# Input stage of a hybrid encoder: order of loads, normalisation and first products

## What is computed

```python
h = layer_norm(x, ln_in_g, ln_in_b)      # (1024, 1024)
p = h @ w_in[0]                          # input projection
# three mixers on parts of p (RWKV-7, neighbourhood attention, latent attention)
# output projection, layer_norm, SwiGLU feed-forward, layer_norm
```

## Time and profile before

| | us |
|---|---|
| median of 3 runs | 1622.75 (1621.57 to 1623.96) |
| the profiled execution | 1622.15 |
| its span | 1620.3 |
| TensorE busy | 1537.1 (95%) |
| VectorE busy | 1074.8 (66%) |
| ScalarE busy | 626.1 (39%) |

### The profile page before, as it was taken

How to read it: one execution, slowest core, us unless ns; L and a number is a source line. 1 busy time by engine, 2 the same in 40 slices (tenths; PEclk the granted TensorE clock), 3 DMA queues, 4 the chain that set the end, 5 groups by cost and what they waited for, 6 DMA issues and landing times.

```text
span 1620.3 us, 25771 instructions
## 1 busy us (share of the span) xinstructions
PE 1537.1 (95%) x10160; PEld 1111.9 (69%) x10160; DVE 1074.8 (66%) x1508; ACT 626.1 (39%) x1157; POOL 360.8 (22%) x360
## 2 busy tenths in 40 slices
PE   4999998989899998999999998999999999998998
PEld 3788784655455545777764456888888888887786
DVE  6524598778756675767647579775555555688877
ACT  2212235655444434444431116333333333343453
POOL 0630004137400017888840050220000000000000
PEclk9999999999999999999999999999999999999999
DMA  6131010010000000000024011332321111755322
GB/s 237 40 152 42 13 53 8 1 33 13 12 12 12 19 11 21 3 2 29 2 77 171 1 52 52 110 111 82 97 95 53 53 53 53 257 197 182 127 69 105
DMA packets 28537, 109.78 MB, mean 68 GB/s; under 512 B 3488, under 2 KB 5888, under 8 KB 26256
## 3 DMA queue, kind: packets, MB, share of 16 engines
q1 hardware_dynamic: 27968, 103.05, 18.8%
q0 software_dynamic: 464, 5.28, 0.9%
HBM read 89.36 MB, written 18.92 MB: 67 GB/s over the span
## 4 chain that ended last, share of the span: by engine, by line
PE 84%; DVE 8%; POOL 3%; issue 2%; ACT 2%; DMA 1%; SPq 0%; DVEq 0%; POOLq 0%; ACTq 0%
PE psum L2746 26%; PE psum L2763 11%; PE psum L2252 9%; PE psum L2669 7%; PE psum L2419 5%; PE psum L2446 3%; PE psum L2343 2%; PE psum L2360 2%; PE psum L2314 2%; PE psum L2281 1%; PE psum L2453 1%; PE psum L2262 1%; PE psum L2643 1%; PE psum L2556 1%; PE psum L2538 1%
## 5 line engine op out<-in xcount | busy, mean ns | idle before, releaser
L2746 PE MATMUL psum<-h_hi,part_hi 128*128 128x512 f32 x616 | 166.3, 392 | 7.9 <-DVE arena L1937 4.6
L1884 DVE TENSOR_TENSOR part_lo<-arena,part_hi 128x512 fp32r<-128x512 f32 x154 | 118.0, 770 | 79.3 <-ACT part_hi L1210 79.0
L2746 PE MATMUL psum<-h_lo,part_hi 128*128 128x512 f32 x616 | 165.4, 390 | 0.0
L2746 PE MATMUL psum<-h_hi,part_lo 128*128 128x512 f32 x616 | 164.7, 389 | 0.0
L1210 ACT ACTIVATE part_hi<-arena 128x512 fp32r<-128x512 f32 x154 | 96.0, 628 | 134.8 <-PE psum L2746 119.1
L2746 PEld LDWEIGHTS psum<-h_hi,part_hi 128*128 128x128 f32 x616 | 115.9, 189 | 33.2 <-DVE arena L1937 5.1
L2746 PEld LDWEIGHTS psum<-h_lo,part_hi 128*128 128x128 f32 x616 | 116.2, 189 | 24.3
L2746 PEld LDWEIGHTS psum<-h_hi,part_lo 128*128 128x128 f32 x616 | 115.7, 188 | 24.1
L893 POOL TENSOR_TENSOR arena<-arena,consts 128x512 f32<-128x512 f32 x64 | 81.7, 1297 | 178.8 <-ACT arena L1114 178.2
L1559 DVE TENSOR_REDUCE stats<-psum 128x1 f32<-128x1024 f32 x64 | 77.8, 1216 | 50.5 <-PE psum L2343 50.4
L2669 PE MATMUL psum<-arena 128*128 128x512 f32 x256 | 110.5, 592 | 0.0
(11 more groups left out here) (322 smaller groups left out, 3078.2 us busy)
## 6 DMA issues: line engine op xcount, KB each, us to landing
arena<-in_w_gate SPq DMA_DIRECT2D x22, 512.0 KB, 3.6
arena<-in_w_up SPq DMA_DIRECT2D x22, 512.0 KB, 4.0
arena<-in_w_down SPq DMA_DIRECT2D x22, 512.0 KB, 3.8
arena<-in_w_down SPq DMA_DIRECT2D x11, 1024.0 KB, 4.9
arena<-in_w_in SPq DMA_DIRECT2D x15, 512.0 KB, 3.5
arena<-act_spill SPq DMA_DIRECT2D x12, 512.0 KB, 7.0
act_spill<-arena SPq DMA_DIRECT2D x10, 512.0 KB, 5.9
arena<-in_x SPq DMA_DIRECT2D x8, 512.0 KB, 11.2
```

The costliest lines, as they stand in the source:

```text
L1884: v.tensor_tensor(lo, raw[:, at:at + HALF], hi, ALU.subtract).then_inc(part_lo, 1)
L2746: mm = pe.matmul(bank({2: z, 3: y, 5: y}.get(p, x)), w[:, P * k:P * k + P], h[k // 2][:, HALF * (k % 2):HALF * (k % 2) + HALF], start=(fre ...
```

## The change

SyncE loads x tiles 0 to 3, each with its own semaphore, then both weight tiles, then x tiles 4 to 7 in pairs, then the constants and the value weights. GpSimd issues the two broadcast rows only when the last x tile is there. Statistics go by pairs of tiles. ScalarE normalises tiles 0, 1, 4 and 6 (by scale and bias, for which VectorE computes minus mean times reciprocal), VectorE 2, 3, 5 and 7. TensorE turns tile by tile, eight blocks each. In the first half ScalarE copies all blocks out, in the second VectorE three of them. VectorE takes the statistics of tiles 4 to 7 between the low parts of the first half. The two weight tiles are interleaved in the first half; in the second half blocks 6 and 7 are turned behind the first products, and the last five products of tile 1 stand behind the last of tile 0. The other edits set the counts of waits further on.

```diff
+IN_BANKS = ((0, 2, 1, 3, 4, 5, 6, 7), (1, 3, 4, 5, 6, 7, 4, 5))
+NORMED_BY_ACT, NORMED_BY_DVE = (0, 1, 4, 6), (2, 3, 5, 7)
+TURNED_BY_DVE = [(1, 1), (1, 4), (1, 7)]
+TURNED_BY_ACT = [(hf, k) for hf in range(NH) for k in range(KT) if (hf, k) not in TURNED_BY_DVE]
+IN_TURNS = (len(TURNED_BY_ACT), len(TURNED_BY_DVE))
...
-            for t in range(NT):
-                sp.dma_start(resid[:, t, :], a["x"][t]).then_inc(rows_in_place[t // 2], 16)
+            for t in range(4):
+                sp.dma_start(resid[:, t, :], a["x"][t]).then_inc(rows_in_place[t], 16)
                 if t == 0:
                     sp.dma_start(ident, a["consts"][:, 0:P]).then_inc(ident_in, 16)
-            sp.dma_start(w_raw[0], a["w_in"][0]).then_inc(weights_in[0], 16)
+            for s in range(NSLOT):
+                sp.dma_start(w_raw[s], a["w_in"][s]).then_inc(weights_in[s], 16)
+            for t in range(4, NT):
+                sp.dma_start(resid[:, t, :], a["x"][t]).then_inc(late_rows_in[t // 2 - 2], 16)
             sp.dma_start(consts[:, P:], a["consts"][:, P:]).then_inc(const_in, 16)
-            sp.dma_start(w_raw[1], a["w_in"][1]).then_inc(weights_in[1], 16)
...
             pool.dma_start(par[:, :], a["params"]).then_inc(par_in, 16)
+            pool.memset(proj[:, 0:NSHIFT, 0:1], 0.0).then_inc(pads, 1)
+            pool.memset(proj[:, 0:NSHIFT, T + 1:T + 2], 0.0).then_inc(pads, 1)
+            pool.wait_ge(late_rows_in[1], 32)
             pool.dma_start(g_row, a["rows"][0:1, :].partition_broadcast(P)).then_inc(rows_in, 16)
             pool.dma_start(b_row, a["rows"][1:2, :].partition_broadcast(P)).then_inc(rows_in, 16)
-            pool.memset(proj[:, 0:NSHIFT, 0:1], 0.0).then_inc(pads, 1)
-            pool.memset(proj[:, 0:NSHIFT, T + 1:T + 2], 0.0).then_inc(pads, 1)
...
-            def sd_in(hf):
-                act.wait_ge(var_ready, hf + 1)
-                act.activation(sd[:, 4 * hf:4 * hf + 4], mv[:, 4 * hf:4 * hf + 4, 1], ACT.Sqrt).then_inc(sd_ready, 1)
+            def sd_in(n):
+                act.wait_ge(var_ready, 2 * n + 1)
+                act.activation(sd[:, 2 * n:2 * n + 2], mv[:, 2 * n:2 * n + 2, 1], ACT.Sqrt).then_inc(sd_ready, 1)
+            def normalise_in(t):
+                act.wait_ge(var_ready, 2 * (t // 2) + 2)
+                act.activation(resid[:, t, :], resid[:, t, :], ACT.Identity, bias=less_means[:, t:t + 1],
+                               scale=rs[:, t:t + 1]).then_inc(norm_act, 1)
...
+            def turn_in(hf, k):
+                if 8 * hf + k >= 4:
+                    act.wait_ge(h_lo_ready, 8 * hf + k - 3)
+                act.wait_ge(ln_tr, 8 * hf + k + 1)
+                act.activation(h_tmp[k % 4], bank(IN_BANKS[hf][k]), ACT.Identity,
+                               bias=pcol("ln_in_b", k), scale=pcol("ln_in_g", k)).then_inc(h_tmp_ready[0], 1)
+            def hi_in(hf, k):
+                turned_in(act, hf, k)
+                act.activation(h_hi[k][:, hf * HALF:(hf + 1) * HALF], h_tmp[k % 4], ACT.Copy).then_inc(h_hi_ready, 1)
+            sd_in(0)
+            normalise_in(0)
+            sd_in(1)
+            normalise_in(1)
+            for j in range(NSLOT):
+                p_hi(j)
+            act.wait_ge(par_in, 16)
+            turn_in(0, 0)
+            turn_in(0, 1)
+            for k in range(KT):
+                hi_in(0, k)
+                if k + 2 < KT:
+                    turn_in(0, k + 2)
+                if k == 5:
+                    sd_in(2)
+            normalise_in(4)
+            sd_in(3)
+            normalise_in(6)
+            turn_in(1, 0)
+            for k in range(KT):
+                hi_in(1, k)
+                if (1, k + 2) in TURNED_BY_ACT:
+                    turn_in(1, k + 2)
...
+            def stats_in(t, j):
+                if t < 4:
+                    v.wait_ge(rows_in_place[t], 16)
+                else:
+                    v.wait_ge(late_rows_in[t // 2 - 2], 32)
+                own.add(v.bn_stats(bn[:, t, 6 * j:6 * j + 6], resid[:, t, j * HALF:(j + 1) * HALF]))
+                if j:
                     own.wait()
                     own.add(v.bn_aggr(mv[:, t, :], bn[:, t, :]))
+            def variance_in(n):
                 own.wait()
...
+                v.tensor_scalar(mv[:, 2 * n:2 * n + 2, 1], mv[:, 2 * n:2 * n + 2, 1], LN_EPS, None, ALU.add).then_inc(var_ready, 1)
+            def scale_in_of(n):
+                v.wait_ge(sd_ready, n + 1)
+                own.add(v.reciprocal(rs[:, 2 * n:2 * n + 2], sd[:, 2 * n:2 * n + 2]))
                 own.wait()
...
+                v.scalar_tensor_tensor(out=less_means[:, 2 * n:2 * n + 2], in0=mv[:, 2 * n:2 * n + 2, 0], scalar=-1.0,
+                                       in1=rs[:, 2 * n:2 * n + 2], op0=ALU.mult, op1=ALU.mult).then_inc(var_ready, 1)
+            def normalise_in(t):
+                v.tensor_scalar(resid[:, t, :], resid[:, t, :], mv[:, t, 0:1], rs[:, t:t + 1],
+                                ALU.subtract, ALU.mult).then_inc(norm_ready, 1)
+            def turn_in(hf, k):
+                v.wait_ge(h_lo_ready, 8 * hf + k - 3)
+                v.wait_ge(ln_tr, 8 * hf + k + 1)
+                v.tensor_scalar(h_tmp[k % 4], bank(IN_BANKS[hf][k]), pcol("ln_in_g", k),
+                                pcol("ln_in_b", k), ALU.mult, ALU.add).then_inc(h_tmp_ready[1], 1)
+            def lo_in(hf, k):
+                v.wait_ge(h_hi_ready, 8 * hf + k + 1)
+                v.tensor_tensor(h_lo[k][:, hf * HALF:(hf + 1) * HALF], h_tmp[k % 4],
+                                h_hi[k][:, hf * HALF:(hf + 1) * HALF], ALU.subtract).then_inc(h_lo_ready, 1)
...
-            for hf in range(2):
-                normalise_in(hf)
-                if hf == 0:
-                    v.wait_ge(par_in, 16)
-                    p_lo(0)
-                for k in range(0, KT, 2):
-                    v.wait_ge(ln_tr, 8 * hf + k + 2)
-                    v.tensor_scalar(h_tmp[k % 4 + 1], bank(5 + k % 4 if hf else k + 1), pcol("ln_in_g", k + 1),
-                                    pcol("ln_in_b", k + 1), ALU.mult, ALU.add).then_inc(h_tmp_ready[1], 1)
-                    for j in range(k, k + 2):
-                        v.wait_ge(h_hi_ready, 8 * hf + j + 1)
-                        v.tensor_tensor(h_lo[j][:, hf * HALF:(hf + 1) * HALF], h_tmp[j % 4],
-                                        h_hi[j][:, hf * HALF:(hf + 1) * HALF], ALU.subtract).then_inc(h_lo_ready, 1)
-                if hf == 0:
-                    p_lo(1)
+            for t in range(2):
+                for j in range(2):
+                    stats_in(t, j)
+            variance_in(0)
+            stats_in(2, 0)
+            scale_in_of(0)
+            stats_in(2, 1)
+            for j in range(2):
+                stats_in(3, j)
+            variance_in(1)
+            scale_in_of(1)
+            for t in range(2, 4):
+                normalise_in(t)
+            for j in range(NSLOT):
+                p_lo(j)
+            for k in range(KT):
+                lo_in(0, k)
+                if 1 <= k <= 4:
+                    stats_in(4 + (k - 1) // 2, (k - 1) % 2)
+                if k == 4:
+                    variance_in(2)
+                elif k == 5:
+                    scale_in_of(2)
+                if k > 4:
+                    stats_in(4 + (k - 1) // 2, (k - 1) % 2)
+            stats_in(7, 1)
+            variance_in(3)
+            normalise_in(5)
+            scale_in_of(3)
+            normalise_in(7)
+            v.wait_ge(par_in, 16)
+            turn_in(1, 1)
+            for k in range(KT):
+                lo_in(1, k)
+                if (1, k + 3) in TURNED_BY_DVE:
+                    turn_in(1, k + 3)
...
+            def normed(t):
+                if t in NORMED_BY_ACT:
+                    pe.wait_ge(norm_act, NORMED_BY_ACT.index(t) + 1)
+                else:
+                    pe.wait_ge(norm_ready, NORMED_BY_DVE.index(t) + 1)
+            def turn_in(hf, t, ks):
+                for k in ks:
+                    mm = pe.transpose(psum[:, IN_BANKS[hf][k], P * (t % 4):P * (t % 4) + P],
+                                      resid[:, t, k * P:(k + 1) * P], ident)
+                    if t % 4 == 3:
+                        mm.then_inc(ln_tr, 1)
+            def first_project(hf, b, k):
                 pe.wait_ge(p_lo_ready, b + 1)
+                pe.wait_ge(h_lo_ready, 8 * hf + k + 1)
                 w_hi_b, w_lo_b = w_parts[b]
...
+                for n, (w, x) in enumerate(((w_hi_b, h_hi), (w_hi_b, h_lo), (w_lo_b, h_hi))):
+                    mm = pe.matmul(bank(2 * b + hf), w[:, P * k:P * k + P], x[k][:, hf * HALF:(hf + 1) * HALF],
+                                   start=(k == 0 and n == 0), stop=(k == KT - 1 and n == 2), skip_group_check=True)
+                if hf and k == KT - 1:
+                    mm.then_inc(proj_done, 1)
             pe.sem_inc(proj_done, NSLOT)
...
+            for t in range(4):
+                normed(t)
+                turn_in(0, t, range(KT))
```

(54 more changed lines are left out.)

53 lines of the change are left out of this document (14 added, 39 removed).

## The result

| | before | after |
|---|---|---|
| median | 1622.34 us (1621.57 to 1623.96, 4 runs) | 1612.37 us (1611.72 to 1613.58, 4 runs) |
| span of the profiled execution | 1620.3 us | 1610.7 us |
| first matmul of weight tile 2 | 60.10 us | 50.19 us |

The ratio is 0.9936, 95% interval 0.9921 to 0.9951: 10.0 us faster. A later comparison on one chip, in which after ran five times beside other kernels, gave 1612.67 against 1620.04 us (11 runs), ratio 0.9956 (0.9943 to 0.9969). Both lie clear of 1, but the second gain is 7.4 us (5 to 9 by its interval) against 10.0 (8 to 13); which is nearer is open.

A forecast was written before the change was run, and what follows sets the result against it. The input stage's chain to weight tile 2's first matmul was taken as the bound, with TensorE waiting on VectorE's normalises. -4.5 - 1.9 - 0.8 - 4.5 + 2.3 = -9.4 (9.5 unrounded): 1622.75 - 9.5 = 1613.2 us, range 1610 to 1618.

The forecast's parts named there:

- to the first turn: Start until ScalarE's first copy of a transposed column out of PSUM: at 17.1 us instead of 21.65, -4.5.
- first turn to first matmul: Two turns, a rounding and a low part before TensorE's first product: 2.8 us instead of 4.7, -1.9.
- first half's products: Sixteen products of 0.70 us and one hole of 0.5: 11.7 us instead of 12.5, -0.8.
- between the halves: TensorE's stretch without products: 5.1 us instead of 9.6, -4.5, with tile 7 normalised and turned last.
- second half's products: Products 11.2 us, eight moved transposes 1.0, a hole 0.5, then a wait of 1.2: 13.9, +2.3.
- Tile 1's landing: x tile 1 in at 6.4 us, behind identity and parameters; bounds 5.8 at the best rate and 9.7 as today.
- The low clock: Seventeen transposes ahead of the first turn priced at 0.24 us each, the 1.2 GHz price, done at 16.9.
- Rival 2: TensorE's clock rises only at 26 us: tile 2 at 53.0; high from the first transpose: 48.7. Chance 0.13.
- The new wait: Weight tile 2 reuses tile 0's parts, freed at its last product: TensorE idle 1.2 us, low part taking 2.48.
- Rival 1: x tiles land as late as today, 9.7 and 13.78: tile 2 starts at 54.4, -5.7; chance 0.12.
- Rival 3: TensorE's clock never rises in the input stage, every matmul 0.47 us: tile 2 at 73.5, +13.4; chance 0.05.
- Rival 4: The gain is given back after the input stage, by other last-ending work or clock dips: about 1621; chance 0.08.

The follow-up runs named there:

- rows_first: after with GpSimd issuing the two row broadcasts at the start again, right behind the parameters; first matmul of weight tile 2 at 52.62 us against 50.19.
- par_late: after with the parameters' load issued only when x tile 1 is in; first matmul of weight tile 2 at 49.86 us against 50.19.
- ident_late: after with the identity loaded behind x tile 3 instead of x tile 0; weight tile 2 at 48.06 us; timed later, median 1610.83 us, ratio 0.9943 to before.
- pool_later: after with GpSimd starting its chain on the normalised rows only when weight tile 2 is split; first matmul of weight tile 2 at 49.83 us against 50.19.
- after_again: The unchanged kernel after, timed and traced a second time; median 1612.67 us, ratio 0.9956 to before, first matmul of weight tile 2 at 49.22 us.
- all_faster: after with identity behind x tile 3, parameters issued once x tile 1 is in, and x tile 5 normalised by ScalarE; median 1612.44 us, ratio 0.9947 to before.
- no_interleave: after with the first half's products as before: all eight blocks with weight tile 0, then with weight tile 1; weight tile 2 at 55.72 us against 50.19.
- warm_start: all_faster plus 18 unread products of a constant tile on TensorE ahead of everything; median 1609.04 us, ratio 0.9930 to before.
- norm_dve: after with all eight x tiles normalised by VectorE, none by ScalarE; first matmul of weight tile 2 at 54.48 us against 50.19.
- weights_late: after with the two weight tiles loaded behind x tiles 4 to 7; first matmul of weight tile 2 at 53.95 us against 50.19.

## Why the prediction was right

Forecast 1613.2 us, measured 1612.4 (a change of -9.5 forecast, -10.0 measured; in the later comparison -7.4); landmark forecast at 50.6, measured 50.19. The sum by its own terms:

| stretch | forecast | measured in after |
|---|---|---|
| to the first turn | -4.5 (at 17.1) | -3.9 (17.78) |
| first turn to first matmul | -1.9 (2.8 us) | -1.9 (2.83) |
| first half's products | -0.8 (11.7) | -0.9 (11.67) |
| between the halves | -4.5 (5.1) | -4.6 (5.03) |
| second half's products | +2.3 (13.9) | +1.3 (12.88) |

Three of the five were right within 0.1 us, since every price in them had a row. Of the two others one came out 0.7 us worse than forecast and one 1.0 better, so that they nearly cancelled: that the landmark came within 0.4 us is partly luck. One of the prediction's own signs of being wrong, a second x tile after 8 us, did show.

*Between the halves* the length is right and the path only in part. The forecast had tiles 4 to 6 turned while VectorE normalised, tile 7 last. VectorE's last normalise ended at 33.3 (forecast 32.9); what set the stretch was TensorE itself, whose products ended at 32.28 (31.6) and whose 24 transposes then took 3.2 us with a short wait for ScalarE's tile 6.

*Tile 1's landing* was put at 6.4 and was 8.28. The term counted the identity and the parameters by their bytes. rows_first shows the broadcasts' part (9.73), par_late and ident_late show the rest (6.53 and 5.70): the two small loads cost far more than their share of bytes. Tile 1 came midway between the forecast and the bound "as today", 9.7, even with the broadcasts gone. The rule of the Trainium skill on turns between queues ("DMA: Bandwidth & Descriptors", section "Queues, rings and completion order"), which I set beside the early bound of 5.8, agrees with rows_first in its direction, 9.73 against 8.28; tile 1 did not come at 5.8 without the broadcasts, since the parameters stayed in the other queue and the identity in the same one, and it was there by 5.70 once the identity had moved.

*The low clock.* From tile 1's landing to the first turn I had 10.7 us, measured 9.5. Transposes were priced at 0.24 throughout; the clock rose under way, and 18 took 3.04 us in the chain where I had 4.1 for 17. Rival 2's "high from the first transpose" was the direction. This saved 1.1 of the 1.9 us lost on the landing.

*The new wait* was there and smaller: 0.33 us for 1.2. Two terms made it so, by about 0.5 us each. "0.6 to the copy out" was mis-sized: I had counted it from where 24 matmuls would have ended without holes, 54.1, while the copy at 54.70 came 0.2 behind the real end, and in after it came 0.19 behind the end of tile 0's last product. The low part took 1.96 for 2.48, between its bounds. That it is GpSimd's work that makes it slow, as the "SBUF — State Buffer" page (section "Terms") of the Trainium skill says of the shared pair, pool_later shows: 1.23 us.

*Rivals.* Rival 1 had nearly its landings in rows_first (tile 1 used at 9.73, tile 3 at 13.99), and the landmark came at 52.62 there, not 54.4. Rival 3, the clock low throughout, did not come; but granted clocks of 0.50 for a stretch within the stage, which no row of before had shown after a hole as short as 2.2 us, came in 6 of the 12 traces of variants (in all six between 17 and 28 us, in three of them also after 40) and cost about 1.1 us where they fell on the second half's products. Rival 4 did not come in these traces: 1560.2 and 1560.5. The later medians, 7.4 us apart, leave room for part of it.

## What to carry to other kernels

A start-up phase is a chain: write its links down with the prices of the trace, and a reordering can be forecast to a microsecond in each stretch (here 0.1 in three of five), least well where it changes who shares the transfer engines. Load first what the first instruction needs and nothing else, small loads in short rows behind it, even if they are few bytes: the identity seemed to be needed first, and moving it behind x tile 3 made the landmark 1.2 and 1.3 us earlier than in after_again. When two products that share a stream of operands are interleaved, the gap that the producer leaves fills, and the producer's own idle slots can take the next phase's preparation; watch that what follows on the same buffers still has its cover.

## What the runs showed of the chip

- 34.5 KB of parameters in rows of 276 bytes, or 64 KB in rows of 512, each held back a 512 KB tile that was queued behind or beside them: with both it was used from 7.49 to 8.30 us (seven traces), without the parameters from 6.53, without the identity from 5.70. From 3 to 7 us the engines moved 251 to 299 GB/s in after, 291 to 393 with the identity out of the way, but 229 to 373 without the parameters, so the rate alone does not explain it.
- Single executions of one kernel differ by up to 7.4 us (all_faster, 1607.80 to 1615.18). TensorE's mean clock goes along roughly: of the eleven runs of before, 0.990 at 1618.55 us and 0.986 at 1623.02, but 0.991 at 1619.93. From the landmark on the traces took 1557.5 to 1564.0 us, with the same instructions.
- The clock went back to 0.50 after holes of 2.2 us in some executions (no_interleave, warm_start) and stayed at 1.00 in others behind the same hole (after, ident_late). In norm_dve and weights_late it fell 0.7 and 1.1 us after the products had begun. What decides it is open.
- Work that nobody reads, 7 us of it ahead of the first transposes, nearly halved their price (1.09 us for eight instead of 1.97).
- A VectorE instruction on 128x2 elements took 2.38 us beside GpSimd's row operation and 0.16 without it.
